# Squares, root and scaling of the gate rows moved into the attention of two blocks

## The reference

```python
def chunk_spatial_gate(u, v, ws, bs):
    vg = v.reshape(B, nc, CHUNK, GMLP_GROUPS, GMLP_GROUP_DIM)
    sv = jnp.einsum('gpq,bnqgc->bnpgc', ws, vg) + bs.T[None, None, :, :, None]
    return u * sv.reshape(B, L, GMLP_WIDTH)

def gqa_attend(q, k, v):
    s = jnp.einsum('bqhgd,bkhd->bhgqk', q, k).astype(jnp.float32) * ATTN_SCALE
    p = jax.nn.softmax(s, axis=-1).astype(v.dtype)
    return jnp.einsum('bhgqk,bkhd->bqhgd', p, v)

# in mixer_merge
a_out = attn @ w_attn_o
gu = jax.nn.gelu(p[..., GU_OFF:GV_OFF])
gv = rms_norm(jax.nn.gelu(p[..., GV_OFF:CG_OFF]), gmlp_norm_g)
g_out = chunk_spatial_gate(gu, gv, gmlp_ws, gmlp_bs) @ w_gmlp_o
c_out = conformer_conv(p[..., CG_OFF:GATE_OFF], ...)
```

## Time and profile before

| | |
|---|---|
| time, median of 3 runs | 4082.25 us (4075.62 to 4085.65) |
| profiled execution, its own time | 4076.49 us |
| its span in the trace | 4074.7 us |
| mean granted TensorE clock | 0.985 of full speed |
| PE (matmul) busy | 3915.8 us, 96% |
| DVE busy | 2245.3 us, 55% |
| ACT busy | 866.7 us, 21% |
| POOL busy | 398.9 us, 10% |
| chain that ended last | PE 87%, DVE 8%, ACT 2%, DMA 2% |

### The profile page before, as it was taken

One profiled execution on the slowest core, in us unless ns is written; L12 is line 12 of the kernel. 1 busy time (PEld: TensorE's weight loads), 2 busy tenths in 40 slices (PEclk: granted clock), 3 DMA queues, 4 the chain that ended last, 5 costly groups with the idle time before them and its releaser, 6 DMA issues.

```text
span 4074.7 us, 35220 instructions
## 1 busy us (share of the span) xinstructions
PE 3915.8 (96%) x12954; PEld 2196.6 (54%) x12954; DVE 2245.3 (55%) x4063; ACT 866.7 (21%) x1735; POOL 398.9 (10%) x254
## 2 busy tenths in 40 slices
PE   7998989999999999999999999999999999899999
PEld 3444555555554555554445444446666457657665
DVE  5893520999204455557215169705666556745666
ACT  2103510000213111113125100113111334432111
POOL 1110000444120000000000023320000001000000
PEclk9999999999999999999999999999999999999999
DMA  7651001111121111111120121222222212002222
GB/s 268 214 199 64 1 26 41 62 41 62 41 69 66 42 62 62 62 62 45 62 83 1 47 83 62 83 79 97 83 83 83 79 53 83 11 21 83 83 87 78
DMA packets 125752, 297.02 MB, mean 73 GB/s; under 512 B 5346, under 2 KB 13586, under 8 KB 125600
## 3 DMA queue, kind: packets, MB, share of 16 engines
q1 hardware_dynamic: 107920, 236.58, 16.5%
q0 software_dynamic: 17680, 58.35, 4.3%
HBM read 292.74 MB, written 2.18 MB: 72 GB/s over the span
## 4 chain that ended last, share of the span: by engine, by line
PE 87%; DVE 8%; ACT 2%; DMA 2%; issue 1%; DVEq 0%; POOL 0%; SPq 0%
PE psum L381 32%; PE psum L2207 30%; PE psum L2259 12%; PE psum L2201 3%; PE psum L1061 2%; PE psum L2304 2%; PE psum L2287 1%; ACT sb_rc L1962 1%; DVE sb_kvt L2562 1%; DVE sb_rc L2562 1%; PE psum L1167 1%; DMA sb_ra<-in_ada_w 1%; DMA sb_ring<-in_ada_w 1%; PE psum L2288 1%; ACT sb_rb L1962 0%
## 5 line engine op out<-in xcount | busy, mean ns | idle before, releaser
L2207 PE MATMUL psum<-sb_ht,sb_ring 128*128 128x512 f32 (+1 forms) x2448 | 892.1, 525 | 0.0
L2207 PEld LDWEIGHTS psum<-sb_ht,sb_ring 128*128 128x128 f32 x2448 | 463.9, 190 | 421.7 <-issue 399.7
L2648 DVE SCALAR_TENSOR_TENSOR sb_rc<-sb_rc,sb_vec x960 | 475.7, 572 | 0.0
L381 PE MATMUL psum<-sb_ring,sb_rc 128*128 128x512 f32 x868 | 392.2, 593 | 7.5 <-DVE sb_rc L527 7.5
L1962 ACT ACTIVATE sb_rc<-psum 128x512 f32<-128x512 f32 (+2 forms) x311 | 155.4, 521 | 1053.0 <-DVE sb_ra L543 294.7
L2259 PE MATMUL psum<-sb_ring,sb_ht 128*128 128x512 f32 x832 | 364.8, 597 | 3.5 <-ACT sb_ht L1962 2.8
L1962 ACT ACTIVATE sb_kvt<-psum 128x512 f32<-128x512 f32 (+4 forms) x214 | 108.2, 532 | 936.0 <-PE psum L2207 761.1
L381 PE MATMUL psum<-sb_ht,sb_ring 128*128 128x256 f32 (+1 forms) x1152 | 306.6, 416 | 0.0
L381 PEld LDWEIGHTS psum<-sb_ring,sb_rc 128*128 128x128 f32 x868 | 164.6, 190 | 216.9 <-issue 204.5
L2207 PE MATMUL psum<-sb_rc,sb_ring 128*128 128x512 f32 (+1 forms) x768 | 276.6, 521 | 4.3 <-ACT sb_rc L1962 2.5
L381 PE MATMUL psum<-sb_rb,sb_rc 128*128 128x512 f32 x588 | 269.6, 595 | 0.0
(11 more groups left out here) (377 smaller groups left out, 4586.9 us busy)
## 6 DMA issues: line engine op xcount, KB each, us to landing
sb_ring<-in_w_in SPq DMA_DIRECT2D x37, 2048.0 KB, 7.9
sb_ring<-in_w_ff SPq DMA_DIRECT2D x32, 2048.0 KB, 8.1
sb_ring<-in_w_ffn SPq DMA_DIRECT2D x16, 2048.0 KB, 7.8
sb_rc<-in_ada_w POOLq DMA_DIRECT2D x26, 1024.0 KB, 5.7
sb_ra<-in_ada_w POOLq DMA_DIRECT2D x14, 1024.0 KB, 5.8
sb_ring<-in_w_gmlp_o SPq DMA_DIRECT2D x4, 2048.0 KB, 7.8
sb_ring<-in_w_attn_o SPq DMA_DIRECT2D x4, 2048.0 KB, 7.8
sb_ring<-in_w_conv_o SPq DMA_DIRECT2D x4, 2048.0 KB, 7.7
```

The lines of the kernel that those rows point to most:

```text
L381: last = pe.matmul(bank(to, width), left[k], right[k], start=k == 0, stop=k == depth - 1)
L2207: last = pe.matmul(bank(b + v, m), ring[:, slot, k, j * P:(j + 1) * P], rhs[:, k, a:a + m], start=k == 0, stop=k == KT - 1)
L2648: step = stt(conv_slot(j, a, m), conv_slot(j + 1, a + k, m), vec[:, j, k:k + 1], conv_slot(j, a, m), op0=ALU.mult, op1=ALU.add)
```

## The change

ACT's squares leave the place between the last gelu and the head copies. Inside the attention, the square of tile u - 2 follows the copy of unit u's probabilities, for u = 2 on, and the root follows unit 3 + n (unit 9 in block 1, unit 7 in block 2). DVE's reciprocal follows unit 11, and the scaling of tile u - 12 follows unit u, for u = 12 on. `ws_raw` and `bs_row` move from `rb` to the columns 2 RD to 2 RD + 1024 of `rc`, the junk area of the squares, and their loads wait for the root (`s_gv_rms`) instead of the last head. The pads lie over those columns, so their clearing waits for DVE's last gate step (`s_sv_ready`) instead of PE's last gate matmul.

```diff
-        ws_raw = rb[:, 0:512].rearrange("p (g q) -> p g q", g=4)
+        ws_raw = rc[:, 2 * RD:2 * RD + 512].rearrange("p (g q) -> p g q", g=4)
         ws_t = rb[:, 1024:1536].rearrange("p (g q) -> p g q", g=4)
-        bs_row = rb[:, 512:1024].rearrange("p (g q) -> p g q", g=4)
+        bs_row = rc[:, 2 * RD + 512:2 * RD + 1024].rearrange("p (g q) -> p g q", g=4)
...
-                pool.wait_ge(*s_att_sb.at(l, OH[l]))
+                pool.wait_ge(*s_gv_rms.at(l, 1))
                 load(ws_raw, t["gmlp_ws"][l].rearrange("g p q -> p g q"), s_ws_in)
                 load(bs_row, t["gmlp_bs"][l:l + 1].to_broadcast([P, 4, P]), s_ws_in)
-
-                pool.wait_ge(*s_sv_ps.at(l, KT))
+                pool.wait_ge(*s_att_sb.at(l, OH[l]))
+
+                pool.wait_ge(*s_sv_ready.at(l, KT))
...
                     fn(PT[:, 0:nk, i * P:(i + 1) * P],
                            bank(4, nk * P).rearrange("p (k n) -> p k n", k=nk)).then_inc(s_att_pt.sem, 1)
+                    if u == 1:
+                        act.wait_ge(*s_gv_sb.at(l, 2 * NT[l]))
+                    if 2 <= u < 2 + NT[l]:
+                        ch.meet()
+                        ch.note(fn(rc[:, 2 * RD:2 * RD + DM], gv_tm[:, u - 2, :], ACT.Square,
+                                   accum_out=ss[:, SG + u - 2:SG + u - 1]))
+                    if u == 3 + NT[l]:
+                        ch.meet()
+                        root(SG, NT[l], DM, s_gv_rms)
...
-                act.wait_ge(*s_gv_sb.at(l, 2 * n))
                 if l == 0:
                     act.wait_ge(*s_late_out.at(0, 16 * LATE))
-                for i in range(n):
-                    ch.link(fn(rc[:, 2 * RD:2 * RD + DM], gv_tm[:, i, :], ACT.Square,
-                               accum_out=ss[:, SG + i:SG + i + 1]))
-                root(SG, n, DM, s_gv_rms)
-
                 for h in range(HEADS + KVH):
...
                     if u + 2 < len(us):
                         peak(u + 2)
+                    if u == 11:
+                        dve.wait_ge(*s_gv_rms.at(l, 1))
+                        reciprocal(SG, NT[l])
+                    if 12 <= u < 12 + NT[l]:
+                        i = u - 12
+                        last = ts(gv_tm[:, i, :], gv_tm[:, i, :], rstd[:, SG + i:SG + i + 1], None, ALU.mult)
+                        if i == NT[l] - 1:
+                            last.then_inc(s_gv_ready.sem, 1)
...
                 normalise_heads(l)
-                dve.wait_ge(*s_gv_rms.at(l, 1))
-                reciprocal(SG, n)
-                for i in range(n):
-                    last = ts(gv_tm[:, i, :], gv_tm[:, i, :], rstd[:, SG + i:SG + i + 1], None, ALU.mult)
-                last.then_inc(s_gv_ready.sem, 1)
                 softmax(l)
```

## The result

| | before | after |
|---|---|---|
| time, median of 5 runs each | 4077.18 us (4074.72 to 4085.65) | 4056.48 us (4054.39 to 4058.28) |
| ratio, 95% interval | | 0.9943 (0.9932 to 0.9954) |
| profiled execution, span | 4074.7 us | 4054.7 us |
| mean granted clock | 0.985 | 0.989 |

The change makes the kernel 0.57% faster; the interval puts it at 0.46 to 0.68%. The two profiled spans differ by 20.0 us. Two more runs of the kernel before moved its median from 4082.25 to 4077.18.

A forecast was written before the change was run, and what follows sets the result against it. PE, busy 96% of the span, was taken to bound the kernel. Gaps 24.8 + clock 8.1 - squares 6.6 - root 2.8 - clock after root 1.7 - scaling 3.2 = 18.6 us off 4082.25: 4063.7, range 4055 to 4077.

The forecast's parts named there:

- The bounds of the sum alone: Whole kernel: gains 24.8 to 32.9 us, costs 9.8 to 19.4, so 5 to 23 saved, 4059 to 4077.
- Gaps and clock: Both ends of both attentions: closing PE's gaps saves 24.8 us, full clock over heads and gate 8.1.
- The rival of the clock not regained: Head turning and gate: gaps close but clock stays low; 10.5 us saved, 4071.8; chance 0.18.
- Squares: Attention units 2, 4, 5, 6 and 2, 4, 5: ACT's squares cost 0.95 us each, 6.6 in all.
- Root: Unit 9 of block 1: root between exponentials needs two table loads, 2.8 us; hidden in block 2.
- clock behind it: Block 1 after the root: PE's gap brings 3.4 us at half speed, costing 1.7 us.
- No drain: Table switches at the root: no drain expected; rival with drain 1.4 us per load, 15.9 saved, 4066.4, chance 0.04.
- Scaling: Units 13, 14, 15, 17 and 13, 14, 15: DVE's scalings cost 0.45 us each, 3.2 in all.
- reciprocal: DVE behind unit 11: its 0.19 us fits in the idle 0.31, so no cost.
- Heads cover: PE's 5 us head-by-v products hide moved work beneath them; rival that they cover nothing: 5.3 saved, 4077.0, chance 0.05.
- Edits at nothing: Old scaling ran beside head copies; POOL's padding, about 2 us later, meets slack before ACT's sigmoid: no cost.
- The slower rival: Attention units with squares: clock falls and stays down, +78 us, net 59 slower, 4142; chance 0.04.

The follow-up runs named there:

- The fill of the gaps: Kernel before, with dummy products of the identity and rows of h, read by nobody, in PE's four gaps; 4073.28 us, ratio 0.9992.
- the fastest version: Changed kernel with squares ahead of head copies, root behind unit 11 (7 in block 2), reciprocal and scalings behind unit 12; 4044.19 us, ratio 0.9918.
- the gap of 5.69: PE's gap in the changed kernel with a tiny exponential and tiny root added behind the root, four table loads per attention; 4062.1 us, one execution.

## What the prediction had right, and the steps that failed

The direction, the places and the mechanism held. The saving was forecast at 18.6 us and is 20.4 by the stages and 20.7 between the medians. The steps that failed are sizes.

The largest is the base. The prediction took its saving off 4082.25, the median of three runs; that of five is 4077.18, 5.1 us lower, and the profiled execution's 4076.5, which the prediction had beside it, was the better guide. In the sum itself it is the price of the squares: each was put at 0.95, the middle of 0.70 and 1.18, so 6.6 us in all, and they cost 5.45. The scalings were put at 3.2 and cost 2.6; the reciprocal was put at nothing and cost 0.22 in each block. All costs together were forecast at 14.3 and are 12.8; the gains were forecast at 32.9 and are 33.2. With the base and the 0.3 between stages and medians this is the way from 4063.7 to 4056.5.

The bounds of the sum alone ended at 4059. The measured time lies inside the stated range only by the 4 us that were added below for the scatter of the runs.

- **Gaps and clock.** Fronts 18.2 measured against 8.6 + 6.2 + 1.7 + 1.8 = 18.3; backs 14.9 against 5.0 + 5.0 + 2.3 + 2.3 = 14.6. The fill of the gaps isolates the clock's share, 8.0 against 8.1.
- **The rival of the clock not regained** fell. In the changed kernel PE does nothing but transposes from 366 to 372.8 and the windows say 1.00; with the gaps filled, these transposes run at full clock too. So the transposes don't cost the clock; idling did. The Trainium skill's rule (TensorE: Matmul & The Clock Gate, part 4 on the PE-mode transpose), that full clock doesn't engage for them, is not what this case's fp32 transposes show.
- **Squares**, 6.6 forecast for seven in the open, measured 5.45 (0.80 + 2.14 + 0.80 + 1.71; by moving them 2.94 + 2.50). This is the mis-sized term: 0.78 each on average, not 0.95. A unit with a square paces at 2.61, so each further square of a run costs 2.61 - 2.18 = 0.43; the run's first, right behind a head's copy, costs 2.14 - 2 x 0.43 = 1.28. The same two prices give block 2's 1.71. Both lie outside the bounds of 0.70 and 1.18 that the prediction gave a single square; that their sum lies inside its bounds is luck, one miss against the other. Why the first costs that much was not tested. The forecast's 2.88 took 1.18 from the chained squares of before and 0.99 for the exponential, where in the loop they take 1.04 and 0.88 from start to start.
- **Root**, 2.8, **and clock behind it**, 1.7: 4.5 forecast, 4.29 measured by taking it away. The gap was 2.66; PE worked some 3.1 us at half clock behind it (416.25 to 419.3), worth about 1.5.
- **No drain.** A switch costs 1.28 and its instruction; two more cost 3.03 together, where the drain would make 5.8. The Trainium skill's extra for a drain (ScalarE: Activation LUTs, "What ACT_TABLE_LOAD costs") does not show here.
- **Scaling**, 3.2 forecast for seven, measured 2.6 (1.16 + 0.30 + 1.15), 0.37 each on average: at the lower bound, for DVE's idle 0.31 a unit was used up in full. Unit by unit it is uneven here too: at the pace of 2.45 a further scaling of a run costs 0.27, which leaves 0.62 for the first, and the lone one behind unit 17 cost 0.30. The one **reciprocal** of unit 11, set at nothing, cost 0.22 in both blocks: it stands ahead of a peak that PE waits for.
- **Heads cover.** The squares of units 3 and 7, the scalings of units 12 and 16 and block 2's root lay under heads in the changed kernel and cost nothing; a square and a root together fitted too. Moving everything there took all costs away.
- **Edits at nothing.** POOL's padding now comes at 540.64 in block 1 and the list of waits has no row of an engine that waits for it. In block 2 the sigmoid's table load starts at 2260.04, 5.4 us behind the last gate step, as it did before.
- **The slower rival** fell: in the stretches with squares the clock stayed at 1.00.

What stays open is the clock outside the altered stages. All ten traces share the code from block 2's gate to the end, and it takes between 1801.7 and 1808.5 us, with 55 to 74 us at half clock: 1802.2 before, 1801.8 after, 1804.7 in the fastest version, 1808.5 with the gaps filled. The time at half goes with it: 55 us in the two traces at 1801.7 and 1801.8, 57 in those at 1802.2 and 1802.7, 61 in the five from 1803.8 to 1804.7, and 74 in the one at 1808.5. Why the clock falls more in one trace than in another, neither the edits nor the idle times explain, and no run tried to.

## What to carry to other kernels

Before moving work off a gap, list the stretches in which its new engine idles because another engine holds the pace, and put it there: the same squares, root and scalings cost 12.8 us one per unit and nothing in blocks under the five microseconds of a head's product. Price work that is added to a busy loop by the start-to-start pace that the engine would reach, not by its busy times, and give the first of a run more than the rest. Where end-to-end times scatter by as much as the edit is worth, compare the stages between two marks: stages with the same code agreed within 0.07 us from trace to trace (136.75 to 136.82 for block 1's attention without the moved work), the clock's falls apart, where the totals moved by several.

## What the runs showed that was not expected

- **When the clock falls is not set by the gap alone.** Behind the gap of 2.66 us it fell 2.3 us after PE's last work (413.6 to about 415.9); behind the gap of 5.69 it was still 1.00 at 418, 4.5 us after it, and fell late in the next microsecond. The time at half, added up from the windows, was 3.4 us in both. So here a gap of twice the length cost its own length and not a longer recovery. Nor does the length alone set the time at half: behind the 4.97 us gap at block 1's gate the clock averaged 0.74 over the 20 us from 520 to 540, which is 10.2 us at half, three times as long as behind the gap of 5.69.
- **The same idle pattern falls on either side.** Three waits of 0.99, 0.99 and 0.90 us at the end of block 2's attention left the clock at 1.00 in seven traces and took it in three: with 5.42 us for the head's product in the former, and 7.11, 7.11 and 7.92 in the latter (gaps filled, scalings under one head, squares under the heads). An execution lost 1.7 to 2.9 us by this with nothing done wrong. A kernel that ends such a stretch with less idle time might be rid of the chance; that was not tried.
